# Down projection: the first trip's banks copied by ScalarE and added to the token rows in the next up phase; a seven-product block more in the second trip

## The reference

```python
h = rmsnorm(x, norm_ffn_g[l])
x = x + jnp.square(jax.nn.relu(h @ w_up[l])) @ w_down[l]
return rmsnorm(x, final_g)
```

## Time and profile before

| | |
|---|---|
| median of 3 runs | 1513.53 us (1513.41 to 1513.58) |
| the profiled execution's own time | 1513.84 us |
| span in the profile (first to last instruction) | 1512.1 us |
| mean granted TensorE clock | 0.999 |
| PE busy | 99% (7636 matmuls) |
| DVE busy | 80% (1607 instructions) |
| ACT busy | 50% (953 instructions) |
| DMA | 290.94 MB, mean 192 GB/s |

### The profile page before, as it was taken

The page is one execution under the profiler, slowest core; times in us unless marked ns, Lnnn a source line. Parts: engine busy times, 40 slices in busy tenths (PEclk is TensorE's granted clock), DMA queues, the critical chain, the costliest instruction groups (busy, mean ns, idle before and its releaser), DMA issues.

```text
span 1512.1 us, 22226 instructions
## 1 busy us (share of the span) xinstructions
PE 1501.1 (99%) x7636; PEld 1265.9 (84%) x7636; DVE 1209.4 (80%) x1607; ACT 763.4 (50%) x953; POOL 2.0 (0%) x11
## 2 busy tenths in 40 slices
PE   9999999999999999999999999999999999999998
PEld 8888888877778888888888888888888888888886
DVE  6668889988889877566876779987799778987797
ACT  6444444465554455444555445544554545544554
POOL 0000000000000000000000000000000000000000
PEclk9999999999999999999999999999999999999999
DMA  8666666655556666666655656655566555656564
GB/s 252 189 184 187 190 193 199 195 180 171 170 171 198 190 200 205 198 194 196 194 182 169 192 195 209 203 182 186 192 201 208 178 194 195 208 181 206 195 215 149
DMA packets 209968, 290.94 MB, mean 192 GB/s; under 512 B 9228, under 2 KB 129108, under 8 KB 209779
## 3 DMA queue, kind: packets, MB, share of 16 engines
q1 hardware_dynamic: 209906, 290.14, 60.6%
HBM read 287.48 MB, written 2.10 MB: 192 GB/s over the span
## 4 chain that ended last, share of the span: by engine, by line
PE 98%; DVE 1%; DMA 0%; ACT 0%; issue 0%; ACTq 0%; DVEq 0%; SPq 0%
PE acc L1367 27%; PE acc L1386 15%; PE acc L1388 15%; PE acc L1387 15%; PE acc L1365 13%; PE acc L1434 3%; PE acc L1435 3%; PE acc L1436 3%; PE acc L1360 2%; PE acc L1460 1%; PE acc L1362 1%; PE acc L1514 0%; PE acc L1536 0%; DMA w_raw<-in_w_down 0%; PE acc L1406 0%; PE acc L1405 0%
## 5 line engine op out<-in xcount | busy, mean ns | idle before, releaser
L537 ACT ACTIVATE w_hi<-w_raw 128x1024 fp32r<-128x1024 f32 x508 | 531.0, 1057 | 466.7 <-PE acc L1388 269.3
L786 DVE TENSOR_TENSOR w_lo<-w_raw,w_hi 128x1024 fp32r<-128x1024 f32 x508 | 612.9, 1221 | 155.4 <-ACT w_hi L537 150.6
L1367 PE MATMUL acc<-h_hl,w_hi 128*128 128x512 f32 x1740 | 546.7, 395 | 0.0
L1365 PEld LDWEIGHTS acc<-h_hl,w_lo 128*128 128x128 f32 x1740 | 322.3, 188 | 72.4 <-issue 0.6
L1365 PE MATMUL acc<-h_hl,w_lo 128*128 128x256 f32 x1740 | 343.6, 279 | 0.0
L1367 PEld LDWEIGHTS acc<-h_hl,w_hi 128*128 128x128 f32 x1740 | 265.2, 189 | 0.0
L1386 PE MATMUL acc<-w_hi,m_hl 128*128 128x512 f32 x424 | 165.3, 390 | 0.0
L1388 PE MATMUL acc<-w_hi,m_hl 128*128 128x512 f32 x424 | 165.0, 389 | 0.0
L1387 PE MATMUL acc<-w_lo,m_hl 128*128 128x512 f32 x424 | 165.0, 389 | 0.0
L1386 PE MATMUL acc<-w_hi,h_hl 128*128 128x512 f32 x384 | 151.5, 394 | 0.0
L1388 PE MATMUL acc<-w_hi,h_hl 128*128 128x512 f32 x384 | 149.6, 389 | 0.0
(11 more groups left out here) (223 smaller groups left out, 1510.4 us busy)
## 6 DMA issues: line engine op xcount, KB each, us to landing
w_raw<-in_w_in SPq DMA_DIRECT2D x200, 512.0 KB, 4.1
w_raw<-in_w_up SPq DMA_DIRECT2D x128, 512.0 KB, 4.5
w_raw<-in_w_down SPq DMA_DIRECT2D x128, 512.0 KB, 4.4
w_raw<-in_w_mix_out SPq DMA_DIRECT2D x32, 512.0 KB, 3.8
w_raw<-in_w_sconv_out SPq DMA_DIRECT2D x16, 512.0 KB, 4.3
w_raw<-in_w_attn_out SPq DMA_DIRECT2D x16, 512.0 KB, 4.1
w_raw<-in_w_conf_out SPq DMA_DIRECT2D x16, 512.0 KB, 4.5
bias_row<-in_gate_b SPq DMA_DIRECT2D x12, 256.0 KB, 4.4
```

The lines of the kernel that those rows point to most:

```text
L537: act.activation(w_hi[:, q], w_raw[:, q], ACT.Copy).then_inc(hi_done, 1)
L786: dve.tensor_tensor(w_lo[:, q], w_raw[:, q], w_hi[:, q].bitcast(F32), ALU.subtract).then_inc(lo_done, 1)
L1365: pe.matmul(*narrow[m], start=False, stop=False)
L1367: last = pe.matmul(*wide[m], start=False, stop=final)
```

## The change

In chunks 0 to 2 the first down trip (t = 0) no longer adds its banks to `y_tok`. ACT copies the corner banks into SBUF (`corner_copies`, two copies of 128x1024 at k = 15, ahead of that step's `hi`), and at k = 0 of the second trip, behind that step's `hi`, the banks P1 and P5 (`p_copies`). DVE, in the same place, makes two sums from P1, P6 and P7 (`partial_sums`). The six adds into `y_tok` come in the next chunk's second up trip, one at each of the steps k = 0 to 5 behind that step's `lo` (`stashed_sum`). That up trip is now written out, and the loop over up trips begins at t = 2. The second down trip (t = 1) of chunks 0 to 2 has a further quad at k = 2, with the order of its first four slabs changed; the weight sums of that quad are begun at k = 14 and 15 of the first trip. Chunk 3 keeps its down phase, but for a wait on `y_acc`. The copies lie in SBUF that the attention and `mix` used before.

```diff
+PAIR_SOON = [(0, 0), (1, 0), (0, 1), (1, 1)] + PAIR[4:]
...
+MIX_QUADS, DOWN_QUADS = 3, 7
+ADDS = 6
...
-    return [(n, i, KDOWN) for n, i in PAIR + PAIR_ENDS[last_trip(ph, c, t)]]
+    return [(n, i, KDOWN) for n, i in (PAIR_SOON if 2 in quads(ph, c, t) else PAIR) + PAIR_ENDS[last_trip(ph, c, t)]]
...
-    return (6,) if last_trip(ph, c, t) else (6, 10, 14)
+    if last_trip(ph, c, t):
+        return (6,)
+    return (2, 6, 10, 14) if t else (6, 10, 14)
+
+def stashed(ph, c, t):
+
+    return ph.name == "down" and t == 0 and not (isinstance(c, int) and c == CHUNKS - 1)
...
         body(PH["up"], c, 0)
-        loop("up", c, first=1)
+        body(PH["up"], c, 1)
+        loop("up", c, first=2)
...
+            def corner_copies(ph, c, t):
+
+                if not (isinstance(c, int) and c == 0 and t == 0):
+                    act.wait_ge(y_acc, ADDS * stash_of(c, t))
+                for n in range(2):
+                    act.wait_ge(c_full, pair_of(ph, c, t) * 2 + (n + 1))
+                    act.activation(corner[n][:, :, :], acc[:, 4 + 2 * n:6 + 2 * n, :], ACT.Copy).then_inc(evac_done, 1)
+
+            def p_copies(ph, c, t):
+
+                act.wait_ge(slab_used, slab_of(ph, c, t, 15) + 1)
+                act.activation(p1_copy[:, :], acc[:, P_BANK["P1"], :], ACT.Copy).then_inc(p_one, 1)
+                act.activation(p5_copy[:, :], acc[:, P_BANK["P5"], :], ACT.Copy).then_inc(p_five, 1)
...
+                    if k == 15 and stashed(ph, c, t):
+                        corner_copies(ph, c, t)
                     hi(ph, c, t, k)
+                    if k == 0 and trip_behind(ph, c, t) and stashed(*trip_behind(ph, c, t)):
+                        p_copies(*trip_behind(ph, c, t))
                     forms_hi(ph, c, t, k)
-                    if quads(ph, c, t) and k == quads(ph, c, t)[-1] + 1:
+                    if quads(ph, c, t) and k == quads(ph, c, t)[-1] + 1 and not stashed(ph, c, t):
                         first_product(ph, c, t, k)
...
+            def partial_sums(ph, c, t):
+
+                g = group_of(ph, c, t, 0)
+                dve.wait_ge(p_one, pair_of(ph, c, t) + 1)
+                dve.wait_ge(p_five, stash_of(c, t) + 1)
+                dve.tensor_tensor(p16[:, :], acc[:, P_BANK["P6"], :], p1_copy[:, :], ALU.add).then_inc(half_sum, 2)
+                dve.wait_ge(half_sum, g + 2)
+                dve.tensor_tensor(p167[:, :], acc[:, P_BANK["P7"], :], p16[:, :], ALU.add).then_inc(p_sum, P_SUMS)
+
+            def stashed_sum(c, step):
+
+                if step == 0:
+                    dve.wait_ge(p_sum, P_SUMS * (pair_of(PH["down"], c, 0) + 1))
+                if not (isinstance(c, int) and c == 0 and step == 0):
+                    dve.wait_ge(y_acc, c * ADDS + step)
+                left, right, both_cols = slice(0, DCOLS), slice(DCOLS, 2 * DCOLS), slice(0, 2 * DCOLS)
+                rows2 = y_tok[:, 1, both_cols].rearrange("p (n w) -> p n w", n=2)
+                dst, src = ((y_tok[:, :, left], corner[0][:, :, :]), (y_tok[:, :, right], corner[1][:, :, :]),
+                            (y_tok[:, 0, left], p1_copy[:, :]), (y_tok[:, :, right], both512(p5_copy)),
+                            (y_tok[:, 0, right], p16[:, :]), (rows2, both512(p167)))[step]
+                dve.tensor_tensor(dst, src, dst, ALU.add).then_inc(y_acc, 1)
...
-                    if k + 3 in quads(ph, c, t):
-                        forms_second(ph, c, t, k + 3)
-                    if k == 15 and paired(ph, c, t):
+                    to, at = (t + 1, k - ph.nslabs) if ph.name == "down" and not t and k >= 14 else (t, k)
+                    if at + 3 in quads(ph, c, to):
+                        forms_second(ph, c, to, at + 3)
+                    if k == 15 and paired(ph, c, t) and not stashed(ph, c, t):
                         corner_sums(ph, c, t)
                     lo(ph, c, t, k)
                     if k == 0 and trip_behind(ph, c, t):
-                        token_sums(*trip_behind(ph, c, t))
-                    if k + 4 in quads(ph, c, t):
-                        forms_first(ph, c, t, k + 4)
+                        (partial_sums if stashed(*trip_behind(ph, c, t)) else token_sums)(*trip_behind(ph, c, t))
+                    if ph.name == "up" and isinstance(t, int) and t == 1 and k < ADDS and not (isinstance(c, int) and c == 0):
+                        stashed_sum(c - 1, k)
+                    if at + 4 in quads(ph, c, to):
+                        forms_first(ph, c, to, at + 4)
```

More of the change, by code:

```diff
@@ L115 @@
 P_SUMS = 5
-MIX_QUADS = 3
+MIX_QUADS, DOWN_QUADS = 3, 7
+ADDS = 6
 def last_trip(ph, c, t):
@@ L136, in quads, with stash_of @@
         return ()
-    return (6,) if last_trip(ph, c, t) else (6, 10, 14)
+    if last_trip(ph, c, t):
[3 more added lines that the diff above has]
+    return ph.name == "down" and t == 0 and not (isinstance(c, int) and c == CHUNKS - 1)
+def stash_of(c, t):
+    return c
 def quad_of(ph, c, t, k):
     at = quads(ph, c, t).index(k)
-    return at if ph.name == "mix" else c * (3 * PH["down"].trips) + t * 3 + (at + MIX_QUADS)
+    return at if ph.name == "mix" else c * DOWN_QUADS + t * 3 + (at + MIX_QUADS)
 def pair_of(ph, c, t):
@@ L159, in trip_behind @@
         return ph, c, t - 1
-    if ph.name == "up" and isinstance(t, int) and not (isinstance(c, int) and c == 0):
+    if ph.name == "up" and isinstance(t, int) and t == 0 and not (isinstance(c, int) and c == 0):
         return PH["down"], c - 1, PH["down"].trips - 1
@@ L307, in build @@
         mix_forms = view("mix_forms", probs, 0, [P, MIX_QUADS, 2, 4, P], F32R)
+        corner = [view(f"corner{n}", probs, 2 * n * DCOLS, [P, 2, DCOLS]) for n in range(2)]
+        p1_copy, p5_copy = (view(f"p{i}_copy", probs, (4 + n) * DCOLS, [P, DCOLS]) for n, i in enumerate((1, 5)))
+        p16, p167 = (view(f"p_{i}", k_dup, n * DCOLS, [P, DCOLS]) for n, i in enumerate(("two", "three")))
         mask = sb("mask", [P, SC])
@@ L359, in build @@
         t_raw, t_two, t_hi, t_lo = sem("t_raw"), sem("t_two"), sem("t_hi"), sem("t_lo")
+        p_five, y_acc = sem("p_five"), sem("y_acc")
         c_full, p_one, p_sum, p_last = sem("c_full"), sem("p_one"), sem("p_sum"), sem("p_last")
@@ L842, in corner_sums @@
             def corner_sums(ph, c, t):
+                if isinstance(c, int) and c == CHUNKS - 1 and t == 0:
+                    dve.wait_ge(y_acc, ADDS * stash_of(c, t))
                 for n in range(2):
```

## The result

The changed kernel is slower: 1516.66 us (median of 11 runs, 1515.02 to 1518.03) against 1513.41 us (11 runs, 1512.49 to 1513.89); ratio 1.0022, 95% interval 1.0014 to 1.0030. I had forecast 1512.1 us, within 1510.8 to 1514.5. The profiled execution has a span of 1515.1 us for 1512.1.

The account below looks back on a forecast made before the run. The prediction took PE's matmul stream, busy 99% of the span, as the bound. Quad -2.04 us plus adds +0.6 us made -1.4 us: 1513.53 to 1512.1 us, called no change, range 1510.8 to 1514.5.

Parts of the forecast that it names:

- Sum and sign: Whole kernel: -2.04 us and +0.6 us give -1.4 us, -0.1%, called no change.
- What is left alone: Up-trip loop turning once fewer with one more trip written out: 0 us; the old 0.56 us wait stays.
- The quad: Second down trips of chunks 0 to 2: nine matmuls fewer on PE, -2.04 us, its forms costing PE nothing.
- The corner copies: ACT, end of the first down trip: 1.06 us each, bounds 0.58 and 1.16, covered by 2 us and more.
- The adds: Six DVE adds in the next chunk's second up trip make PE wait 0.2 us, three times: +0.6 us.
- just in time: Second up trip: a DVE result ending at X for a matmul due at M costs PE X + 0.16 - M.
- The waits at the first quads: Where up goes over into the first down trip: 0.56 us of PE wait stays, or may go if loads fall better.
- the adds are hidden: Rival, second up trip: adds cost nothing, 1511.5 us, or 1510.9 with the old wait gone too; chance 0.18.
- adds late: Rival: adds make PE wait for DVE's `lo` in the second up trip, 1515.4 us at the upper bound; chance 0.14.
- new quad waiting: Rival: the new quad's sums wait on a load, 1.0 us in each of three trips, 1515.1 us; chance 0.10.

Follow-up runs that it names:

- e1: Changed kernel, but on PE alone the second up trip stays in the loop over up trips; 1511.9 us, ratio to the kernel before 0.9986.
- e4: e1 without the further quad at k = 2, copies, sums and adds kept; 1513.47 us, ratio to the kernel before 0.9998.
- e3: Kernel before the change, with the second up trip written out on ACT, DVE and SP but not PE; 1513.95 us, ratio 1.0001.
- e6: Kernel before the change, with 144 idle semaphore increments in PE's body of the chunk loop (1478 instructions); 1513.79 us, ratio 0.9995.
- f7: Changed kernel with PE's chunk loop moved by 63 instructions, a quarter of a block; 1512.32 us, ratio to the kernel before 0.9986.
- e9: Changed kernel with 128 idle increments on PE ahead of the chunk loop, moving it half a block; 1513.1 us, ratio to the kernel before 0.9993.
- e5: Changed kernel with the loop over chunks 1 and 2 written out on every engine; 1511.64 us, ratio to the kernel before 0.9985.
- f3: Changed kernel with PE's chunk loop moved by 255 instructions, a whole block less one; 1518.06 us, ratio to the kernel before 1.0024.

## Why the prediction was wrong

- **Sum and sign.** Forecast -1.4 us, measured +3.3. The step that failed is the one under "What is left alone": "The loop over up trips turns one time fewer and one more trip is written out; the rows show no PE time at such borders, and "issue" has 0% of the chain: 0." It was worth +5.3 us in the profile, 5.4 by e1: PE's longer loop body, 8 blocks in place of 6 or 7, was fetched again at the jump back over a chunk. The rows did show no PE time at the borders, but of a program that fitted; they could not say what the same border costs a longer one. The rival that was missing is one more term, and it is on the other side of the sum.
- **The quad: right.** Nine matmuls fewer, 0.68 us for each of three trips in the starts; by itself some 2 us (e1 against e4, 1.6 by the medians, 2.1 by the starts). No wait at the new quad.
- **The corner copies: right within bounds.** They took 1.02 us each, where I took 1.06 and bounded by 0.58 and 1.16; the page "VectorE: DVE Perf Modes" of the Trainium skill, section "The TRN2 errata", gave an estimated 1.00.
- **The adds: mechanism right, price too high.** DVE's times came out to a tenth, and PE did wait for `w_lo` in that trip, but the term of 0.6 us (0.4 for two chunks) was several times too large. The group that should lose 0.06 lost 0.04 (11.21 us for 11.17) and the next one 0.01; the up phases of chunks 1 and 3 together are 0.06 us longer, in e1 all three together 0.02 us, and e4 can't be told from the kernel before. The 0.16 us that I put on "just in time" came from matmuls of 512 columns; here the first one behind the wait has 256, which may be why it is less.
- **The waits at the first quads** (rival "the adds are hidden", with the old wait gone): they were absent in the changed kernel's profile, present in part in e3, e4 and e6, and 1.4 us in e9. At the first quad of chunk 1, e1 lost 0.1 us and f7 0.3. They go with how long DVE waits for the load (1.5, 2.4 and 3.2 us, above), but no run controls that, so the 0.8 us that the changed kernel gained here was luck. e5 and f7 lose about 1 us at the second quad of chunk 3, where PE waits for `w_forms`.
- **The two rivals on the slow side** (adds late, new quad waiting) did not occur. 1516.66 lies outside the range, near what the first of them gives, for a reason that neither had.

What stays open: the loss at the jump is 3.5 us in one profile and 6.0 in another. Between f3 (3.5) and the changed kernel (5.3) the holes are the same, 3.5 and 3.6 us, and the rest is the clock, which stays at 1.00 behind f3's; why it falls behind one and not behind the other, no run shows. Nor do they show what makes 8 touched blocks too many. The section of "Runtime: NRT & Kernel Launch" of the Trainium skill named above gives PE's store as 128 KiB, eight blocks, filled as a FIFO ahead of use, so that a body of 8 blocks should just fit. That the block beyond the jump is fetched ahead of use as a ninth and pushes out the head would explain it, and in the changed kernel a packet of q8 does move between 1155 and 1156 us, ahead of the jump. No run tests that apart.

The best versions are those that keep the change and lose the hole: e1 (0.9986), e5 (0.9985) and f7 (0.9986), 1.8 to 2.5 us below the kernel before. Of these e1 is the one to keep, since its body is the shortest.

## What to carry to other kernels

Writing a loop's trip out is an edit of its own on every engine whose queue it lengthens, even when the work stays the same. Count the engine's instructions between an outer loop's head and its jump back, in blocks of 256, before and after; here PE paid 5 us once the body touched 8 blocks, and PE could keep the trip in its loop while DVE, ACT and SP had it written out (e1). When a gain is 0.1%, a term put down as 0 "because the rows show none" deserves the question whether the changed kernel is still the one that the rows describe; q8's packet count on the page answers it at a glance.

## What the runs showed of the hardware

- In all 11 kernels of the table, PE keeps the body of the loop across the jump back where it touches at most 7 blocks of 256 instructions (by the fitted start), and where it touches 8, q8 moves 9 more packets of 16 KB. The same body of 1603 instructions costs 0 or 3.5 to 5.3 us, by where it starts (f7 and e9 against the changed kernel and f3).
- A straight program of 11728 PE instructions (e5) streams in with 46 packets and no wait of PE for issue in the chunks.
- Behind the holes of 3.6 us in the changed kernel's matmul stream the granted clock averaged 0.55 over 3.8 us; behind f3's, 3.5 us, it stayed at 1.00.
- An ACT copy of 128x1024 from PSUM takes 1.02 us.
